# Modulation vectors of the first two tiles computed tile by tile, with the first weight chunk loaded between their two row pairs

## The reference

```python
mod_x = (silu(c) @ w_mod + b_mod)              # 6 vectors of 1024: sh1, sc1, gt1, sh2, sc2, gt2
mod_c = silu(c_ctx) @ w_mod + b_mod            # the same for the 256 context tokens
h_x = rmsnorm(x, g_pre_mix) * (1 + sc1) + sh1  # and h_c from ctx with csc1, csh1
p   = h_x @ w_in                               # first large matmul, contraction over 1024 = 8 tiles of 128
```

## Time and profile before

| | us |
|---|---|
| median of 3 runs (1344.57 to 1345.51) | 1344.88 |
| the profiled execution, its own time | 1345.02 |
| its span in the trace | 1343.7 |
| PE busy in the span | 1333.6 (99%) |
| DVE / ACT / POOL busy | 572.3 / 558.6 / 629.3 |

### The profile page before, as it was taken

How to read it: one execution, slowest core, us unless ns; L and a number is a source line. 1 busy time by engine, 2 the same in 40 slices (tenths; PEclk the granted TensorE clock), 3 DMA queues, 4 the chain that set the end, 5 groups by cost and what they waited for, 6 DMA issues and landing times.

```text
span 1343.7 us, 16536 instructions
## 1 busy us (share of the span) xinstructions
PE 1333.6 (99%) x6610; PEld 1077.4 (80%) x6610; DVE 572.3 (43%) x921; ACT 558.6 (42%) x933; POOL 629.3 (47%) x333
## 2 busy tenths in 40 slices
PE   9999999999999999999999999999999999999999
PEld 6788778888888888888788887776878888888887
DVE  5796786653200152103477657665532221122211
ACT  4522675554432244224565548544542231222220
POOL 3544326944444444555476553642444444344442
DMA  9675235432323333233342112111233233322331
GB/s 380 240 285 200 89 144 188 151 106 83 94 94 101 102 101 97 94 98 117 103 122 63 48 63 66 61 47 48 64 94 94 94 96 108 94 94 94 94 110 62
DMA packets 41228, 150.70 MB, mean 112 GB/s; under 512 B 4288, under 2 KB 4544, under 8 KB 40384
## 3 DMA queue, kind: packets, MB, share of 16 engines
q1 hardware_dynamic: 40272, 146.36, 32.9%
q0 software_dynamic: 448, 2.62, 0.5%
q10 hardware_dynamic: 432, 0.67, 0.1%
HBM read 146.75 MB, written 2.10 MB: 111 GB/s over the span
## 4 chain that ended last, share of the span: by engine, by line
PE 92%; DVE 4%; ACT 2%; DMA 1%; issue 1%; POOL 1%; SPq 0%; DVEq 0%; ACTq 0%; POOLq 0%
PE bank L597 26%; PE bank L599 25%; PE bank L598 25%; PE bank L674 2%; PE bank L1033 2%; PE bank L644 1%; PE bank L645 1%; PE bank L646 1%; PE bank L689 1%; PE bank L658 1%; PE bank L841 1%; PE bank L682 1%; PE bank L822 1%; DVE small L2158 1%; DMA xq<-in_xt 1%
## 5 line engine op out<-in xcount | busy, mean ns | idle before, releaser
L2719 POOL TENSOR_TENSOR wL<-raw,wH 128x1024 fp32r<-128x1024 f32 (+1 forms) x209 | 509.7, 2441 | 573.1 <-ACT wH L1341 570.0
L597 PE MATMUL bank<-hH,wH 128*128 128x512 f32 x784 | 317.0, 404 | 1.3 <-POOL wL L2719 0.6
L599 PE MATMUL bank<-hH,wL 128*128 128x512 f32 x784 | 305.8, 390 | 0.0
L598 PE MATMUL bank<-hL,wH 128*128 128x512 f32 x784 | 305.7, 390 | 0.0
L1341 ACT ACTIVATE wH<-raw 128x1024 fp32r<-128x1024 f32 (+1 forms) x209 | 219.4, 1051 | 191.0 <-PE bank L599 164.0
L597 PEld LDWEIGHTS bank<-hH,wH 128*128 128x128 f32 x784 | 147.4, 188 | 38.2 <-issue 7.1
L599 PEld LDWEIGHTS bank<-hH,wL 128*128 128x128 f32 x784 | 147.2, 188 | 31.8
L598 PEld LDWEIGHTS bank<-hL,wH 128*128 128x128 f32 x784 | 147.5, 188 | 28.8 <-issue 1.9
L597 PE MATMUL bank<-gH,wH 128*128 128x512 f32 x352 | 137.6, 391 | 0.0
L599 PE MATMUL bank<-gH,wL 128*128 128x512 f32 x352 | 137.0, 389 | 0.0
L598 PE MATMUL bank<-gL,wH 128*128 128x512 f32 x352 | 136.9, 389 | 0.0
(11 more groups left out here) (388 smaller groups left out, 1904.4 us busy)
## 6 DMA issues: line engine op xcount, KB each, us to landing
raw<-in_wall SPq DMA_DIRECT2D x209, 512.0 KB, 3.6
rows<-in_wall SPq DMA_DIRECT2D x24, 1024.0 KB, 11.3
bra<-in_rpbw SPq DMA_DIRECT2D x8, 360.0 KB, 4.3
xq<-in_xt SPq DMA_DIRECT2D x2, 1024.0 KB, 7.1
xT<-in_xn SPq DMA_DIRECT2D x1, 2048.0 KB, 7.9
out_x<-xT SPq DMA_DIRECT2D x8, 256.0 KB, 2.5
vE<-in_ctxt SPq DMA_DIRECT2D x1, 1024.0 KB, 20.6
icn<-in_invc POOLq DMA_DIRECT2D x1, 1024.0 KB, 8.6
```

Source lines behind the costliest of these rows:

```text
L597: matmul(o, a_h, b_h, start=first, stop=False)
L598: matmul(o, a_h, b_l, start=False, stop=False)
L599: return matmul(o, a_l, b_h, start=False, stop=last)
L2719: tt(wL[i % NHL][:, 0:n], raw[i % NRAW][:, 0:n], wH[i % NHL][:, 0:n].bitcast(F32), ALU.subtract).then_inc(s.w_lo, 1)
```

## The change

Tiles 0 and 1 get parts of their own. The first two chunk pairs of `w_mod` are laid out so that a pair holds shift and scale of a single tile for all eight k, where before a pair held half of the k for both tiles. There are then five parts: part 0 is tile 0, part 1 is tile 1, parts 2 to 4 are tiles 2 and 3, 4 and 5, 6 and 7.

```diff
+        if quarter == 0:
+            plan.extend(("w_mod", k, 8 * sec + j, True) for j in range(2) for k in range(8) for sec in range(2))
+            continue
...
+def vectors_of(j):
+    return j + 1 if j < 2 else j // 2 + 2
...
         def first_rows(p):
+            place, part = ROW_PLACE[p], p if p < 2 else p // 2 + 1
             pe.wait_ge(row_in[place], 16 * row_turn(p))
             pe.wait_ge(s.silu_c, 1)
+            pe.wait_ge(s.mod_row, part if p else 0)
+            if p < 2:
+                for k in range(8):
+                    c, i = divmod(k, 4)
+                    mm = matmul(bank[5 + p][32 * i:32 * i + 32, 0:256], cond[:, k, :],
+                                rows_[place][:, c, 256 * i:256 * i + 256], start=c == 0, stop=c == 1)
...
+        def first_columns(part):
+            b = 4 if part == 0 else 7
+            o = claim(b)
             pe.wait_ge(s.sel, 3)
+            pe.wait_ge(s.mod_row, part + 1)
+            for j in range(2 if part < 2 else 4):
...
         mm.then_inc(s.summed, 1)
         freed[7] = s.root, logged("x")
+
+        first_columns(0)
+        for j in (0, 2):
+            matmul(bank[0], ones[:, :], xsq[:, j, :], start=True, stop=True)
         first_rows(1)
-
-        matmul(bank[0], ones[:, :], xsq[:, 0, :], start=True, stop=True)
-        first_columns(0)
-        for j in (2, 4):
-            matmul(bank[0], ones[:, :], xsq[:, j, :], start=True, stop=True)
-        freed[6] = s.mod_row, 4
+        matmul(bank[0], ones[:, :], xsq[:, 4, :], start=True, stop=True)
+        freed[5], freed[6] = (s.mod_row, 1), (s.mod_row, 5)
...
         def other_quarters(k, m):
+            if (k, m) in ((1, 0), (2, 3), (3, 1)):
+                first_rows(2 * k)
+                first_rows(2 * k + 1)
+            if (k, m) in ((0, 1), (1, 2), (2, 5), (3, 5)):
+                first_columns(k + 1)
...
         def first_norm(j):
-            act.wait_ge(s.coef_a, j // 2 + 1)
+            act.wait_ge(s.coef_a, vectors_of(j))
...
+        def first_vectors(part):
+            n, b = (256, 5 + part) if part < 2 else (512, 6)
+            dve.wait_ge(s.mod_mm, part + 1 if part < 2 else 2 * part)
+            dve.wait_ge(s.mod_col, max(0, part - 1))
+            nc.vector.tensor_copy(mrow[part % 2][:, 0:n], bank[b][:, 0:n]).then_inc(s.mod_row, 1)
...
+        def first_tile(j):
+            i = j % 2
+            n = normed("x", j - i)
+            dve.wait_ge(s.coef_a, vectors_of(j))
+            dve.wait_ge(s.x_scaled, j + 1)
+            dve.wait_ge(s.rest_g if i else s.rest_v, REST.first + n)
+            o = tm[i][:, :] if j else bank[3]
+            ts(o, xq[:, j, :], coef[:, 0, j:j + 1], mod[:, j, 0:1], ALU.mult, ALU.add).then_inc(s.full, 1)
+            if i == 0:
+                dve.wait_ge(s.hi, HI.first + 2 * n + 1)
+                dve.wait_ge(s.full, FULL.first + 2 * n + 1)
+                rest(hL[:, j, :], o, hH[:, j, :], s.rest_v)
...
         first_vectors(0)
+        first_coefficients(0)
         dve.wait_ge(s.root, rooted("x"))
         scaled(0)
+        first_tile(0)
+        first_vectors(1)
         scaled(1)
-        first_coefficients(0)
-        first_norm(0)
+        first_coefficients(1)
+        first_tile(1)
         scaled(2)
         scaled(3)
-        first_vectors(1)
+        first_vectors(2)
         for j in range(4, 8):
             scaled(j)
-        first_coefficients(1)
+        first_coefficients(2)
         first_norm(1)
...
+        pool.wait_ge(s.x_scaled, 1)
         ahead("w_in", 0, 0, 1)
         first_rest("x", 1)
...
-        rows_load(0, 1)
+        rows_load(0)
         weights_load(0)
+        rows_load(1)
         weights_load(1)
```

More of the change, by code:

```diff
@@ L694, in first_rows @@
         def first_rows(p):
-            quarter, half = divmod(p, 2)
-            place = ROW_PLACE[p]
+            place, part = ROW_PLACE[p], p if p < 2 else p // 2 + 1
             pe.wait_ge(row_in[place], 16 * row_turn(p))
             pe.wait_ge(s.silu_c, 1)
[L699 to L702, removed]
+            pe.wait_ge(s.mod_row, part if p else 0)
[4 more added lines that the diff above has]
+                                rows_[place][:, c, 256 * i:256 * i + 256], start=c == 0, stop=c == 1)
+            else:
+                half = p % 2
+                for i in range(4):
+                    mm = matmul(bank[6][32 * i:32 * i + 32, :], cond[:, 4 * half + i, :],
+                                rows_[place][:, i // 2, 512 * (i % 2):512 * (i % 2) + 512], start=half == 0,
+                                stop=half == 1)
             mm.then_inc(s.mod_mm, 1)
-        def first_columns(quarter):
-            o = claim(7)
+        def first_columns(part):
+            b = 4 if part == 0 else 7
+            o = claim(b)
             pe.wait_ge(s.sel, 3)
-            pe.wait_ge(s.mod_row, quarter + 1)
-            for j in range(4):
-                mm = matmul(o[:, 2 * j:2 * j + 2], mrow[quarter % 2][:, 128 * j:128 * j + 128], sel[:, 2, :], start=True,
+            pe.wait_ge(s.mod_row, part + 1)
+            for j in range(2 if part < 2 else 4):
+                mm = matmul(o[:, 2 * j:2 * j + 2], mrow[part % 2][:, 128 * j:128 * j + 128], sel[:, 2, :], start=True,
                             stop=True)
             mm.then_inc(s.mod_col, 1)
-            freed[7] = s.coef_a, quarter + 1
+            freed[b] = s.coef_a, part + 1
         def late_column(sec, j, at_=0):
@@ new lines, in first_coefficients @@
+        def first_coefficients(part):
+            f0, w = (part, 1) if part < 2 else (2 * part - 2, 2)
+            o = bank[4] if part == 0 else STAT
+            shift, scale = [o[:, 2 * w * i:2 * w * i + 2 * w].rearrange("p (j c) -> p j c", c=2) for i in range(2)]
+            dve.wait_ge(s.mod_col, part + 1)
+            tt(mod[:, f0:f0 + w, :], shift, view(vcs("b_mod"), f0, [[1, w], [0, 2]]), ALU.add).then_inc(s.mod_ab, 1)
+            tt(scale, scale, view(vcs("b_mod"), 8 + f0, [[1, w], [0, 2]]), ALU.add).then_inc(s.mod_ab, 1)
+            dve.wait_ge(s.mod_ab, 2 * part + 2)
+            stt(out=view(coef[:, 0, f0:f0 + w], 0, [[8, 2], [1, w]]),
+                in0=view(o, 2 * w, [[1, 2], [2, w]]), scalar=1.0,
+                in1=view(vcs("g_pre_mix"), f0, [[0, 2], [1, w]]), op0=ALU.add, op1=ALU.mult).then_inc(s.coef_a, 1)
@@ L2055, in scaled @@
         def scaled(j):
             tt(xq[:, j, :], xq[:, j, :], rs[0][:, :], ALU.mult).then_inc(s.x_scaled, 1)
-        def first_norm(quarter):
[L2060 to L2074, removed]
+        def first_tile(j):
[10 more added lines that the diff above has]
+                rest(hL[:, j, :], o, hH[:, j, :], s.rest_v)
@@ L2076, in context_norm @@
+        def first_norm(quarter):
+            first_tile(2 * quarter)
+            first_tile(2 * quarter + 1)
         def context_norm(j0):
@@ L2108, in vector_program @@
             tt(acc[1][:, 0:256], acc[1][:, 0:256], tm[2 + j % 2][:, 0:256], ALU.add).then_inc(s.add_v, 1)
-        first_vectors(2)
-        first_coefficients(2)
+        first_vectors(3)
+        first_coefficients(3)
         first_norm(2)
-        first_vectors(3)
+        first_vectors(4)
         context_norm(0)
-        first_coefficients(3)
+        first_coefficients(4)
         first_norm(3)
```

## The result

The changed kernel takes 1347.45 us (median of 20 executions, 1346.56 to 1349.29), the kernel before 1345.05 us (20 executions, 1344.36 to 1346.10): a ratio of 1.0020, 95% interval 1.0014 to 1.0026, 2.4 us slower. The median hides two groups. Twelve executions have a mean granted clock of 1.000 and take 1346.56 to 1347.98 us (median 1346.88); eight have 0.999 and take 1348.27 to 1349.29 us (median 1349.05). The first group alone is 1.8 us slower than the kernel before. The 63 executions of the kernel before that were taken beside experiments e1 to e8 all have 1.000. The profiled execution is of the first group: 1346.61 us, span 1345.3 us.

The account below looks back on a forecast made before the run. PE was taken as the bound (busy 1333.6 of 1343.7 us). Start -0.36, columns +0.40, k=1 +0.3, k=2 +1.0 and columns at (2,5) +1.2 gave +2.54, hence 1347.4 us; range 1345.4 to 1348.7.

Parts of the forecast that it names:

- S: Start of PE's first product: claimed at 19.64 us instead of 20.00, 0.36 us gained.
- my 0.10 for weight loads: At `first_rows(0)`: 0.10 us added for extra weight loads of eight 256-column matmuls, over the old sets' 1.00 us.
- rival A: Start not gained: low half keeps 2.84 us or `first_rows(0)` costs up to 0.8 more; 1347.9 to 1348.6; chance 0.25.
- The low half: POOL's low half of chunk 0, before the first product: claimed 2.37 us instead of 2.84, ending at 19.50.
- The wait at k=1: PE waiting for POOL's hL of tile 1 at k=1: claimed about 0.3 us.
- the wait at k=2: PE waiting for DVE's hL of tile 2 at k=2: claimed 1.0 us of new wait.
- modulation of tile 2: DVE's modulation of tile 2: claimed to start at 30.93 us instead of 28.39, 2.54 us later.
- Rival D: Second tile's rest on POOL held behind two multiplications, or chunk 1 late: 0.6 to 1.0 more at k=1; 1348.2; chance 0.10.
- The columns at (2,5): Claimed to start at 40.52 us, 2.54 later than 37.98, with PE waiting 1.73 us instead of 0.50.
- B: Context additions slip past POOL's low half of chunk 2, PE itself sets the columns at 38.79: +0.8, 1345.7; chance 0.12.
- C: Not slower: the DVE chain up to the columns at (2,5) is wholly hidden; 1344.9, down to 1344.4; chance 0.08.
- Nothing gives it back: After the columns at (2,5) the same work in the same order remains, so the +2.54 us reaches the end.

Follow-up runs that it names:

- e1: The changed kernel with the rows of tiles 2 and 3 put back behind (0,3): 1347.34 us, against 1344.78 for the kernel before; ratio 1.0017.
- e8: The kernel before with only DVE's copy of the rows of tiles 4 and 5 moved to behind the fourth context addition: 1344.23 us, ratio 0.9995.
- e4: The changed kernel with DVE's multiplication of tile 1 put back directly behind that of tile 0: 1348.58 us over 7 executions, against 1344.78.
- e5: The changed kernel with DVE's copy for the columns at (2,5) moved ahead of three context additions: 1345.17 us, ratio 1.0004 to the kernel before.
- e6: The changed kernel with its parts kept, but rows, columns and coefficients back in the old places: 1344.48 us, ratio 0.9997 to the kernel before.
- e3: The kernel before with three more filler matmuls between the first columns and the first product: 1346.70 us, against 1344.78.
- e2: The changed kernel with five small matmuls filling PE's wait ahead of the columns at (2,5): 1346.61 us, against 1344.78 for the kernel before.

## Why the prediction was right, and where it was not

**Start.** Forecast S = 19.64, measured 19.53, with an execution that was 0.06 us early at the sums. `first_rows(0)` in four sets took 1.00 us as before: my 0.10 for weight loads was not there, nor was any of rival A. The low half took 2.37 us, the value taken, not 2.84, and the low halves of chunk 1 bear out the reason (under e4).

**Tile 1 and the next rows.** The columns cost 0.36 in the stream (20.99 to 21.35), forecast 0.40. The wait at k=1 was 0.13, not 0.3; the wait at k=2 0.73, not 1.0; modulation of tile 2 at 30.71, not 30.93. Between S and that step it is 11.18 us, forecast 11.29. Rival D did not come: chunk 1's low half ended at 27.09, before the products of (1,2).

**The columns at (2,5).** Forecast 40.52, measured 40.30, 2.32 us later than before against a forecast of 2.54; the wait there 1.63, forecast 1.73. Neither B nor C came about, since the context additions kept their place against POOL's low half (2.44 us again). e5 shows that this wait is DVE's copy standing behind additions that it doesn't need, and e6 that with the old places the delay is gone. So the mechanism of the forecast was right up to here.

**"Nothing gives it back"** is the step that failed, though the total came out. Two terms of the sum were missing, of opposite sign. First, something is given back: the columns are 2.3 us late, but the group that kept its clock (1346.88 us) is only 1.8 above the kernel before. In the traces 0.7 us is given back at the first attention, by the medians 0.5, and for e3's plain shift the medians show nothing; so that this shift as such gives it back isn't shown. Second, the clock: the wait that I had priced at its own length lets the granted clock fall in 8 of 20 executions, which take 1349.05 us at their median, 2.2 above the others. The fall in e4's trace cost 1.5 us; that the rest of the 2.2 belongs to the same cause isn't shown. The median of the mixture lies at the forecast 1347.4 by luck of that mixture, and a single profiled execution (1346.61) would have put it 0.8 below. The forecast's own wait of 1.73 us was the sign: in the kernel before no wait of PE from the first product to the columns is longer than 0.6 us (at the first product), and I asked what the new one cost in time and not what it cost in clock.

The forecast's sum with measured terms: start -0.47, columns +0.36, waits at k=1, k=2 and (2,5) +0.13, +0.73 and +1.13 (1.63 less the 0.50 of before) make +1.88. Of the other 0.4 to the 2.32, 0.3 lies in three starts that are 0.1 us later than the pace, each right behind the columns of tile 1 or a wait (24.35 to 24.69, for one); the last 0.1 is not located.

## What to carry to other kernels

When a step is made smaller and earlier, follow the instruction after it: here the first tile gained 0.47 us, and the steps of the next tiles, pushed behind it, brought the columns at (2,5) 2.3 us late through a chain on another engine that had only 0.5 us of slack. Look for the copy or small step that stands behind work it does not need, before moving anything larger: moving one DVE copy took all but 0.3 us of the loss back and, together with the old places, gave the fastest of these kernels. Repeat a kernel whose PE has got a new wait and look at the granted clock of every execution, since one profile can miss a second group 2 us away.

## What the runs showed that I had not expected

A PE wait of about 1.5 us goes with a loss of clock in some executions and not in others: in 8 of 20 executions of the changed kernel, 8 of 11 of e1 and 6 of 7 of e4, and in none of 66 of e2, e3 and e5 to e8, where no such wait is left in the trace. One trace, e4's, shows where it happens: the mean granted clock is 0.80 from 40.6 to 42 us, 0.50 from 42 to 44 and 0.79 from 44 to 46. The changed kernel's own profiled execution had a wait of 1.47 us and kept 1.00. One execution of e1 has 0.997 and takes 1348.99 us, 3.3 above those that kept their clock; no trace shows what happened in it.

Sixteen records of 256 columns (`first_rows(0)` now) took 1.00 us to the start of what follows, exactly as eight records of 512 before: with 32-column weights the extra loads cost nothing here.
